# Two-block transformer on one core: the work ahead of the last attention is dealt out between units of weight products

## The reference

```
h  = adaln(stream, kv_norm, shift, scale)          # rmsnorm, then a gain and a shift per feature
kv = (h @ w_kv).reshape(b, s, 6, 4, 64)            # k_c, v_c, k_s, v_s, k_w, v_w
def compress(t, pe, w1, w2):                       # 31 overlapping blocks of 32 tokens, per head
    blk = t[:, idx] + pe                           # idx[n] = 16 n + (0 .. 31)
    return silu(blk.reshape(.., 31, 32 * 64) @ w1) @ w2
k_cmp, v_cmp = compress(k_c, ..), compress(v_c, ..)
k_sel, k_win = partial_rope(k_s, pos), partial_rope(k_w, pos)
h    = adaln(x, norm_pre_mix[1], sh_m, sc_m)       # the same stream, another gain and shift
proj = h @ w_q                                     # queries (1024) and branch gates (48)
# then: compressed scores, branch gates, rotated queries, selected and window attention, @ w_o
```

## Time and profile before

| | |
|---|---|
| median of 3 runs | 2889.33 us (2885.91 to 3405.5) |
| the profiled execution: its own time | 2894.63 us |
| its span, first to last instruction | 2893.0 us |
| mean granted TensorE clock | 0.958 of full |
| TensorE busy | 2615.4 us, 90% of the span |
| VectorE, ScalarE, GpSimd busy | 1353.5, 1073.9, 206.6 us |

### The profile page before, as it was taken

One profiled execution on the slowest core, in us unless ns is written; L12 is line 12 of the kernel. 1 busy time (PEld: TensorE's weight loads), 2 busy tenths in 40 slices (PEclk: granted clock), 3 DMA queues, 4 the chain that ended last, 5 costly groups with the idle time before them and its releaser, 6 DMA issues.

```text
span 2893.0 us, 35173 instructions
## 1 busy us (share of the span) xinstructions
PE 2615.4 (90%) x13316; PEld 2116.0 (73%) x13316; DVE 1353.5 (47%) x1869; ACT 1073.9 (37%) x1569; POOL 206.6 (7%) x249
## 2 busy tenths in 40 slices
PE   6978788898999989898899999998797888999999
PEld 5855577677887877685478888887684666788887
DVE  5765377467654364423544333343515444433323
ACT  2235322214453144334644333232314554433322
POOL 1101111010000010001201000010001111100000
PEclk9979899899999999998999999999888999999999
DMA  6730174324323222221012322323210000123232
GB/s 243 265 113 1 59 262 151 125 74 162 127 87 109 95 61 73 88 73 44 1 61 65 110 92 94 102 88 103 69 59 15 15 22 7 66 88 101 80 102 87
DMA packets 178690, 263.19 MB, mean 91 GB/s; under 512 B 8232, under 2 KB 127904, under 8 KB 178592
## 3 DMA queue, kind: packets, MB, share of 16 engines
q1 hardware_dynamic: 156608, 194.00, 20.5%
q0 software_dynamic: 15232, 58.72, 5.7%
q10 hardware_dynamic: 6752, 9.09, 0.9%
HBM read 255.51 MB, written 2.10 MB: 89 GB/s over the span
## 4 chain that ended last, share of the span: by engine, by line
PE 72%; DVE 12%; ACT 7%; issue 5%; POOL 3%; DMA 1%; ACTq 0%; DVEq 0%; SPq 0%; POOLq 0%
PE ps L689 19%; PE ps L690 19%; PE ps L691 19%; PE ps L1270 2%; DVE wlo L2058 2%; PE ps L914 2%; ACT decay L1864 1%; PE ps L956 1%; DVE macc L2075 1%; PE ps L1375 1%; ACT pnt_h L1953 1%; DVE pnt_l L2062 1%; PE ps L1190 1%; ACT whi L1495 1%; DVE actl L2062 1%
## 5 line engine op out<-in xcount | busy, mean ns | idle before, releaser
L2058 DVE TENSOR_TENSOR wlo<-raw,whi 128x2048 fp32r<-128x2048 f32 x180 | 412.1, 2290 | 751.1 <-ACT whi L1495 750.9
L689 PE MATMUL ps<-acth,wlo 128*128 128x512 f32 (+1 forms) x1888 | 702.4, 372 | 29.2 <-DVE actl L2062 17.7
L690 PE MATMUL ps<-actl,whi 128*128 128x512 f32 (+1 forms) x1888 | 697.6, 369 | 0.0
L691 PE MATMUL ps<-acth,whi 128*128 128x512 f32 (+1 forms) x1888 | 697.3, 369 | 0.0
L1495 ACT ACTIVATE whi<-raw 128x2048 fp32r<-128x2048 f32 x180 | 343.7, 1910 | 593.8 <-PE ps L691 593.8
L689 PEld LDWEIGHTS ps<-acth,wlo 128*128 128x128 f32 x1888 | 358.7, 190 | 93.0 <-DVE actl L2062 15.4
L691 PEld LDWEIGHTS ps<-acth,whi 128*128 128x128 f32 x1888 | 358.1, 190 | 60.3
L690 PEld LDWEIGHTS ps<-actl,whi 128*128 128x128 f32 x1888 | 358.8, 190 | 58.7
L689 PE MATMUL ps<-whi,hid_l 128*128 128x512 f32 x528 | 207.8, 394 | 5.2 <-DVE conv_t L2286 3.4
L690 PE MATMUL ps<-wlo,hid_h 128*128 128x512 f32 x528 | 206.0, 390 | 0.0
L691 PE MATMUL ps<-whi,hid_h 128*128 128x512 f32 x528 | 205.9, 390 | 0.0
(11 more groups left out here) (329 smaller groups left out, 3709.6 us busy)
## 6 DMA issues: line engine op xcount, KB each, us to landing
mraw<-in_mod_w POOLq DMA_DIRECT2D x48, 1024.0 KB, 5.6
raw<-in_ffn_w_in SPq DMA_DIRECT2D x44, 1024.0 KB, 4.9
raw<-in_ffn_up SPq DMA_DIRECT2D x22, 1024.0 KB, 4.9
raw<-in_ssm_w_in SPq DMA_DIRECT2D x20, 1024.0 KB, 5.1
raw<-in_ffn_w_out SPq DMA_DIRECT2D x20, 1024.0 KB, 4.9
raw<-in_sb_win SPq DMA_DIRECT2D x12, 1024.0 KB, 5.0
raw<-in_ffn_down SPq DMA_DIRECT2D x10, 1024.0 KB, 4.9
raw<-in_xa_wkv SPq DMA_DIRECT2D x8, 1024.0 KB, 5.2
```

Source lines behind the costliest of these rows:

```text
L689: nc.tensor.matmul(o, ll, rh, start=start, stop=False, skip_group_check=True)
L690: nc.tensor.matmul(o, lh, rl, start=False, stop=False, skip_group_check=True)
L691: return nc.tensor.matmul(o, lh, rh, start=False, stop=stop, skip_group_check=True)
L2058: nc.vector.tensor_tensor(wlo[:, slot, :], raw[:, slot, :], whi[:, slot, :].bitcast(F32), ALU.subtract) \
```

## The change

Arithmetic and weights are the same. What changes is the order on three engines, and the place of one buffer.

- TensorE does four duplications behind bank 1 and four behind bank 3 of the second feature pair, in place of all eight behind the value units. It waits for the small parameters (`nsa_in`) before that pair.
- The four row-turning blocks stand one each ahead of the four units of the first compression layer.
- The four key rotations stand one each behind the four banks of the first pair of queries, and the second compression layer (`compressed_heads`) behind bank 1 of the second pair of queries. The wait for `cmp_kept` stands behind that pair.
- ScalarE makes the high parts of the blocks (`blocks`) behind the feature copies; it modulates a block ahead of each unit's split and Silu; it copies queries bank by bank, with the rotated keys between them (`query_copies`), and loads the gate weights behind bank 1 of the second query pair.
- VectorE writes the blocks between the splits of the value units, modulates one block per compression unit, and does the table products and the rotated low parts between the splits of the query units.
- `kcph` moves from the place of `acth` to the first two parts of the arena (there the halves of `kcph` lie in the place of the spent `pn` and of chunks 0 to 3 of `kv8`), and `kcpl` lies in the place of `kcp`, since `acth` and `actl` are now written while the blocks are still read.

```diff
@@ -345,8 +345,8 @@
     assert o <= arena_end, (o, arena_end)
-    kcph = place("kcph", [P, 2, 16, KV * N_CMP], F32R, at=ACTS)
-    kcpl = place("kcpl", [P, 2, 16, KV * N_CMP], F32R, at=ACTS + 16384)
+    kcph = [place(f"kcph{w}", [P, 16, KV * N_CMP], F32R, at=ARENA + 16384 * w) for w in range(2)]
+    kcpl = place("kcpl", [P, 2, 16, KV * N_CMP], F32R, at=ARENA + 49152)
     rotary = place("rotary", [P, 2, SEQ], at=WIDE)
@@ -703,7 +703,7 @@
-        def feature_turn(ah, al, n=SEQ, free=bank_free):
+        def feature_turn(ah, al, n=SEQ, free=bank_free, behind={}):
@@ -717,6 +717,8 @@
                     last.then_inc(marks, 1)
+                    if (u, j) in behind:
+                        behind[u, j]()
@@ -1115,34 +1117,41 @@
+        def rotate_chunk(c, mats):
+            pe.wait_ge(rot_in, turns(rot_in, 2))
+            for keep, move in mats:
+                if rotated[0] >= 4:
+                    pe.wait_ge(rot_free, rotated[0] - 3)
+                o = ps[:, 4 + rotated[0] % 4, :]
+                nc.tensor.matmul(o, keep, rot_t[:, c % 2, 0, :], start=True, stop=False)
+                nc.tensor.matmul(o, move, rot_t[:, c % 2, 1, :], start=False, stop=True).then_inc(rot_ready, 1)
+                rotated[0] += 1
         def rotate(chunks, mats):
...
             for c in range(chunks):
-                pe.wait_ge(rot_in, turns(rot_in, 2))
-                for keep, move in mats:
-                    if rotated[0] >= 4:
-                        pe.wait_ge(rot_free, rotated[0] - 3)
-                    o = ps[:, 4 + rotated[0] % 4, :]
-                    nc.tensor.matmul(o, keep, rot_t[:, c % 2, 0, :], start=True, stop=False)
-                    nc.tensor.matmul(o, move, rot_t[:, c % 2, 1, :], start=False, stop=True).then_inc(rot_ready, 1)
-                    rotated[0] += 1
-        def compression():
-            for n in range(2 * KV):
+                rotate_chunk(c, mats)
+        def duplicates(first):
+            for n in range(first, first + KV):
                 if n >= 4:
...
                     .then_inc(dup_ready, 1)
+        def compression():
             pe.wait_ge(dup_free, 2 * KV)
-            rotate(4, [(select[:, half, :], select[:, 2 + half, :]) for half in range(2)])
-            banks_out()
             for w in range(2):
-                pe.wait_ge(blocks_lo, w + 1)
                 for u in range(2):
+                    turn_block(2 * w + u, None, norm_diag)
+                    if (w, u) == (0, 0):
+                        banks_out()
+                    if u == 0:
+                        pe.wait_ge(blocks_lo, w + 1)
                     pe.wait_ge(unit_ready, SLOTS + turns(unit_ready))
@@ -1150,12 +1159,15 @@
                             last = product3(ps[:, 2 * w + j, 0:KV * N_CMP], wh[:, k, c], wl[:, k, c],
-                                            kcph[:, w, KC * u + k, :], kcpl[:, w, KC * u + k, :],
+                                            kcph[w][:, KC * u + k, :], kcpl[:, w, KC * u + k, :],
                                             u == 0 and k == 0, u == 1 and k == KC - 1)
...
             turns(bank_free, 4)
-            banks_out()
+            turns_out()
+        def compressed_heads():
             pe.wait_ge(rot_free, rotated[0])
@@ -1165,7 +1177,6 @@
             last.then_inc(cmp_ready, 1)
-            pe.wait_ge(cmp_kept, 1)
@@ -1464,15 +1475,15 @@
         first_pair(branch_out, scaled)
-        feature_pairs(1, acth, actl)
-        value_units()
         banks_out()
         pe.wait_ge(nsa_in, 16 * NSA_PARAMS)
+        feature_turn(acth, actl, behind={(0, 1): lambda: duplicates(0), (1, 1): lambda: duplicates(KV)})
+        value_units()
         compression()
-        for t in range(TB):
-            turn_block(t, None, norm_diag)
-        turns_out()
-        feature_pairs(2, acth, actl)
+        halves = [(select[:, half, :], select[:, 2 + half, :]) for half in range(2)]
+        feature_turn(acth, actl, behind={(c // 2, c % 2): lambda c=c: rotate_chunk(c, halves) for c in range(4)})
+        feature_turn(acth, actl, behind={(0, 1): compressed_heads})
+        pe.wait_ge(cmp_kept, 1)
         banks_out()
@@ -1908,22 +1919,25 @@
-        def rotated_out(dst, banks):
-            for b in range(banks):
+        def rotated_out(dst, banks, first=0):
+            for b in range(first, first + banks):
                 act.wait_ge(rot_ready, turns(rot_ready))
...
-        def compression():
+        def blocks():
             for w in range(2):
...
                 act.wait_ge(dup_free, KV * w + KV)
-                nc.scalar.activation(kcph[:, w, :, :], kcp[:, w, :, :], ACT.Copy).then_inc(blocks_hi, 1)
-            rotated_out(kdup_h, 2 * KV)
+                nc.scalar.activation(kcph[w][:], kcp[:, w, :, :], ACT.Copy).then_inc(blocks_hi, 1)
+        def compression(gain, shift):
             act.wait_ge(hid_padded, 2)
             for w in range(2):
+                modulated_block(acth, 2 * w, gain, shift)
                 act.wait_ge(marks, turns(marks))
                 split(0)
+                modulated_block(acth, 2 * w + 1, gain, shift)
                 for j in range(2):
@@ -1932,6 +1946,25 @@
                 split(1)
+        def query_copies(pair, behind):
+            for b in range(4):
+                act.wait_ge(marks, turns(marks))
+                nc.scalar.activation(q_u[:, 4 * pair + b, :], ps[:, b, :], ACT.Copy, scale=0.125).then_inc(bank_free, 1)
+                if b % 2:
+                    split(b // 2)
+                behind(b)
+        def gate_weights(b):
+            if b == 1:
+                act.wait_ge(cmp_kept, 1)
+                act.dma_start(w_gate[:], a["nsa_w_q_2"][0].rearrange("(k p) c -> p k c", p=P)[:, :, D:]) \
+                    .then_inc(gate_w, 16)
+            if b == 3:
+                act.wait_ge(gate_w, 16)
+                nc.scalar.activation(w_gate_h[:], w_gate[:], ACT.Copy).then_inc(gate_hi, 1)
@@ -2012,6 +2045,7 @@
         feature_copies(2, kv8)
+        blocks()
@@ -2019,16 +2053,11 @@
         split(1)
-        compression()
-        act.wait_ge(cmp_kept, 1)
-        act.dma_start(w_gate[:], a["nsa_w_q_2"][0].rearrange("(k p) c -> p k c", p=P)[:, :, D:]).then_inc(gate_w, 16)
-        act.wait_ge(gate_w, 16)
-        nc.scalar.activation(w_gate_h[:], w_gate[:], ACT.Copy).then_inc(gate_hi, 1)
-        modulated_his(acth, *modulation(1, 48))
+        compression(*modulation(1, 48))
+        query_copies(0, lambda b: rotated_out(kdup_h, 2, 2 * b))
+        query_copies(1, gate_weights)
         act.dma_start(rotary_q[:], a["c_rotary"].rearrange("p (n c) -> p n c", n=2)).then_inc(rotary_in, 16)
-        feature_copies(2, q_u, 0.125)
         act.wait_ge(c_args, 1)
@@ -2477,27 +2506,31 @@
-        def rotate(src, chunks, outputs, hi, lo, table):
-            def split_out(c):
-                for n in range(outputs * c, outputs * c + outputs):
-                    dve.wait_ge(rot_hi, turns(rot_hi))
-                    bank = 4 + (turns.seen["rot_hi"] - 1) % 4
-                    lo_part(lo[:, n, :], ps[:, bank, :], hi[:, n, :]).then_inc(rot_free, 1)
-            for c in range(chunks):
+        def rotate_in(src, c, table):
+            for n in range(2):
+                nc.vector.tensor_tensor(rot_t[:, c % 2, n, :], src[:, c, :], table[:, n, :], ALU.mult) \
+                    .then_inc(rot_in, 1)
+        def rotate_out(c, outputs, hi, lo):
+            for n in range(outputs * c, outputs * c + outputs):
+                dve.wait_ge(rot_hi, turns(rot_hi))
+                bank = 4 + (turns.seen["rot_hi"] - 1) % 4
+                lo_part(lo[:, n, :], ps[:, bank, :], hi[:, n, :]).then_inc(rot_free, 1)
+        def rotate_queries():
+            for c in range(KC):
                 if c >= 2:
...
-                    split_out(c - 2)
-                for n in range(2):
-                    nc.vector.tensor_tensor(rot_t[:, c % 2, n, :], src[:, c, :], table[:, n, :], ALU.mult) \
-                        .then_inc(rot_in, 1)
-            split_out(chunks - 2)
-            split_out(chunks - 1)
-        def compression():
+                    rotate_out(c - 2, 1, acth, actl)
+                rotate_in(q_u, c, rotary_q)
+            rotate_out(KC - 2, 1, acth, actl)
+            rotate_out(KC - 1, 1, acth, actl)
+        def duplicates(first):
             dve.wait_ge(nsa_in, 16 * NSA_PARAMS)
-            for n in range(2 * KV):
+            for n in range(first, first + KV):
                 w, g = n // KV, n % KV
@@ -2510,16 +2543,26 @@
                 last.then_inc(dup_free, 1)
-            for w in range(2):
-                dve.wait_ge(blocks_hi, w + 1)
-                lo_part(kcpl[:, w, :, :], kcp[:, w, :, :], kcph[:, w, :, :]).then_inc(blocks_lo, 1)
+        def compression():
+            for t in range(TB):
+                scaled(1, 48)(t)
+                split(t % 2)
+            turns(marks, 6)
+            keys = kv8[:, 4:8, :]
+            rotate_in(keys, 0, rotary)
```

(33 more changed lines are left out.)

## The result

The changed kernel takes 2854.64 us (median of 4 runs, 2854.42 to 2855.21) against 2889.82 us before (4 runs): 35.2 us less, ratio 0.9883, 95% interval 0.9864 to 0.9902. One of the four runs before took 3405.5 us in a slow state and is left out of the ratio; the median of the other three is 2889.33 us. The forecast was 2856, within 2847 to 2874.

What follows compares the result with a forecast made beforehand. TensorE, on the chain of waits for 72% of the span, bounds the kernel; 141.4 us work + 0.7 + 0.8 waits = 142.9 against 175.8, 32.9 saved, so 2856 us against the median; range 2847 to 2874.

Steps and rivals of the forecast that it cites:

- The stretch: From the second pair of key/value features to the first compressed score: 142.9 us forecast against 175.8 before, 32.9 saved.
- duplications: Eight duplication matmuls on TensorE: 7.4 us of work, from 3.70 for the first four in the old profile.
- rotation: Key rotation on TensorE: 16 matmuls at a spacing of 0.86 us, 13.8 us of work.
- eight query banks: Query products on TensorE: eight banks, copied out every 5.44 us, 43.5 us of work.
- Heads: Second compression layer on TensorE: bounds 4.3 and 2.2 us; 2.2 taken, since they stand behind a full-clock query bank.
- Rival 1: Compression products and turned blocks: clock falls to 1.2 GHz, 29.4 us more, only 3.5 saved, time 2886; chance 0.04.
- The value copies: Behind the value units: end about 1.3 us later, under the first turned block of 1.9 us, so cost nothing.
- Duplications covered by 45 us of products: What fed the 22.7 us duplication stage is hidden behind products; without that cover it would cost 10.8 us again.
- First rotation wait: Behind query bank 0, ending at 2053.5: TensorE waits for the first rotation input, ready at 2054.2, a 0.7 us stall.
- The helpers' room: Each 7.4 us compression step: ScalarE 5.3, VectorE 5.1 us; low parts ready 4 to 5 us before their product.
- rival 2: Compression: ScalarE and VectorE run one after the other, 9.1 us a step instead of 7.4; saved 18, time 2872; chance 0.12.
- Nothing behind the stretch: After the first compressed score: no order changes, so the whole saving carries to the end of the kernel.

Runs made afterwards that it cites:

- Heads back: Changed kernel with the second compression layer moved back ahead of the queries, right behind the compression products: 2857.8 us (4 runs), stretch 141.8 us.
- Row turning back: Changed kernel with all four row-turning blocks together behind the compression products again: 2883.3 us (10 runs), stretch 171.7 us.
- row turning back but for one block: Changed kernel with one row-turning block ahead of the compression products and the other three behind them: 2864.5 us (2 runs), stretch 150.8 us.

## Why the prediction was right, point by point

- **The stretch, 142.9 forecast, 141.8 measured.** The work was forecast at 141.4 and came as 140.6. Single terms were off and cancelled: duplications 6.1 for 7.4, rotation 12.2 for 13.8, but the eight query banks 45.8 for 43.5. In part this is only where one group is cut from the next, as products start under the end of a rotation: a rotation with its query bank takes 8.89 us, forecast 3.44 + 5.44 = 8.88. For the duplications the prediction took the length of a record, 3.70, where the distance to the next work is 3.03.
- **Heads, 2.2 taken between 2.2 and 4.3:** 2.15 measured at clock 1.00. Heads back shows that the place behind a query bank was not needed for it: in its profiled execution they cost the same ahead of the queries.
- **The clock held.** Rival 1 (0.04) did not come about: the new group changes, which the rule of the Trainium skill cited with it speaks against (page TensorE: Matmul & The Clock Gate, section A second HAM failure mode: psum-queue depth-cycling), left 141.8 us at 1.00. That rule asks for brief idle times between the groups as well, and the new order has only two, 0.4 and 0.8 us, so this is hardly a test of it. The prediction took the clock for a property of the products, from rows in which they ran at 1.00. Row turning back shows that the same products can run at 0.50 nearly throughout, which costs 17.8 us. The prediction valued the turned block ahead of them as cover for the value copies and not for the clock: in this it was lucky.
- **The value copies "under the first turned block": nothing.** Right, and this block was worth more than I wrote: without it there are 1.5 us of idle time, and the products behind them cost 17.8 us more at half clock.
- **Duplications covered by 45 us of products:** right; uncovered they cost 11.9, with waits of 5.0, 2.3 and 1.4 us.
- **First rotation wait 0.7:** 0.4 measured. **The helpers' room:** right for the weights' low parts, and rival 2 did not come about; for the turned rows no room was laid out, and they are ready just 0.06 us ahead.
- **Nothing behind the stretch:** 0.6 us in the profiled pair, within the scatter of these runs.

The parts do not add up to the whole: 11.9 + 8.3 + 9.1 + 0.0 = 29.3 of 34.0 when one is undone at a time (with row turning back but for one block), and 50 with row turning back in full, which loses the clock. What each is worth depends on what stands around it.

## What to carry to other kernels

List the work of the bounding engine at its full rate and take the difference to the stretch as the gain to be had; then look only at the places where a helper's result must be there first. Cover short waits ahead of a long run of narrow matmuls, and look at the clock behind each gap: here 1.5 us of idle time stood ahead of 17.8 us lost at half clock, while 0.8 us at another place cost only itself. Where small matmuls contract over 64 rows, each with its own weights, let neighbours in the queue use different halves of the rows.

## What the runs showed of the hardware that was not expected

- 192 products of 124 columns, back to back: 21.4 us at 2.4 GHz when entered from a turned block without a gap, 39.7 us when entered behind 1.5 us of idle time, at 1.2 GHz from 2 us on to their end, although TensorE was never idle in them.
- Score matmuls of 64 rows x 32 columns, at 1.2 GHz in both cases but for the first 2 us: 24.6 us for 64 with neighbours on the same half of the rows, 12.3 us with neighbours on different halves.
- Wide products dealt between such narrow ones did not hold the clock: it fell 4 us behind the first narrow group, and three 512-column products went from 0.90 to 1.57 us from start to start.
